# Sums over the partitions as two single-pass products in a hybrid decoder trunk, with the first values kept in DRAM

## What is computed

```python
for l in range(DEPTH):
    h = rms_norm(x, norm_g[l]).astype(x.dtype)
    p = h @ w_in[l]
    z, p_rw, p_ml, p_mla, p_da = _split(p, IN_WIDTHS)
    v_res = None if l == 0 else (rw_v0[l - 1], rw_v_dn[l - 1], rw_v_up[l - 1])
    y_rw, v_first = rwkv7_group(p_rw, v_first, rw_mu[l], ...)
    y_ml = mlstm_group(p_ml, ...)
    y_mla = mla_group(p_mla, ...)
    y_da = diff_attn_group(p_da, l, ...)
    y = jnp.concatenate([beta[0] * y_rw, beta[1] * y_ml, beta[2] * y_mla, beta[3] * y_da], axis=-1)
    y = y * jax.nn.silu(z.astype(jnp.float32))
    x = x + (y.astype(x.dtype) @ w_out[l]).astype(x.dtype)
```

## Time and profile before

| what | value |
|---|---|
| time, median of 3 runs (range) | 2308.97 us (2307.95 to 2311.85) |
| span of the profiled execution | 2306.3 us |
| PE busy | 2270.2 us, 98% |
| POOL busy | 1744.8 us, 76% |
| DVE busy | 1079.8 us, 47% |
| ACT busy | 662.4 us, 29% |
| granted PE clock | 0.998 of full speed |
| mean DMA rate | 125 GB/s |

### The profile page before, as it was taken

One profiled execution on the slowest core, in us unless ns is written; L12 is line 12 of the kernel. 1 busy time (PEld: TensorE's weight loads), 2 busy tenths in 40 slices (PEclk: granted clock), 3 DMA queues, 4 the chain that ended last, 5 costly groups with the idle time before them and its releaser, 6 DMA issues. The chain is left out here.

```text
span 2306.3 us, 38356 instructions
## 1 busy us (share of the span) xinstructions
PE 2270.2 (98%) x16032; PEld 1736.0 (75%) x16032; DVE 1079.8 (47%) x1411; ACT 662.4 (29%) x1193; POOL 1744.8 (76%) x1228
## 2 busy tenths in 40 slices
PE   7999999999999999999999999999999999999999
PEld 5767777777777778777777677767777777777777
DVE  5023337456463762555250232465474547626542
ACT  5222222222221332443341233222132213314421
POOL 3677679678587999888537666886696789898884
PEclk9999999999999999999999999999999999999999
DMA  4722344333234545733445232523332345466333
GB/s 161 191 85 78 108 142 118 92 96 105 81 108 135 160 150 174 252 91 78 146 114 165 82 105 78 174 86 95 94 115 89 88 156 158 135 201 225 90 82 124
DMA packets 165487, 288.64 MB, mean 125 GB/s; under 512 B 28792, under 2 KB 36344, under 8 KB 163776
## 3 DMA queue, kind: packets, MB, share of 16 engines
q1 hardware_dynamic: 125216, 211.60, 31.4%
q10 hardware_dynamic: 40096, 74.57, 9.9%
HBM read 234.43 MB, written 51.68 MB: 124 GB/s over the span
## 5 line engine op out<-in xcount | busy, mean ns | idle before, releaser
L752 POOL TENSOR_SCALAR w_hi<-raw 128x512 fp32r<-128x512 f32 x552 | 908.1, 1645 | 360.9 <-PE ps_proj L793 311.8
L762 POOL TENSOR_TENSOR w_lo<-raw,w_hi 128x512 fp32r<-128x512 f32 (+1 forms) x640 | 842.4, 1317 | 153.5 <-ACT w_hi L1247 98.1
L793 PE MATMUL ps_proj<-h_hi,w_hi 128*128 128x512 f32 (+1 forms) x1760 | 726.1, 413 | 5.1 <-ACT stage L1240 2.4
L793 PE MATMUL ps_proj<-h_lo,w_hi 128*128 128x512 f32 (+1 forms) x1760 | 688.9, 391 | 0.0
L793 PE MATMUL ps_proj<-h_hi,w_lo 128*128 128x512 f32 x1728 | 675.4, 391 | 0.0
L793 PEld LDWEIGHTS ps_proj<-h_hi,w_hi 128*128 128x128 f32 (+1 forms) x1760 | 329.6, 187 | 101.0 <-issue 22.4
L793 PEld LDWEIGHTS ps_proj<-h_lo,w_hi 128*128 128x128 f32 (+1 forms) x1760 | 329.4, 187 | 73.5 <-DVE h_lo L1769 0.2
L793 PEld LDWEIGHTS ps_proj<-h_hi,w_lo 128*128 128x128 f32 x1728 | 325.8, 189 | 66.2 <-issue 7.7
L808 PE MATMUL ps_proj<-w_hi,h_hi 128*128 128x512 f32 x448 | 181.0, 404 | 0.4 <-POOL w_lo L762 0.4
L808 PE MATMUL ps_proj<-w_hi,h_lo 128*128 128x512 f32 x448 | 174.8, 390 | 0.0
L808 PE MATMUL ps_proj<-w_lo,h_hi 128*128 128x512 f32 x448 | 174.6, 390 | 0.0
(11 more groups left out here) (349 smaller groups left out, 2972.1 us busy)
## 6 DMA issues: line engine op xcount, KB each, us to landing
raw<-in_w_in_dram SPq DMA_DIRECT2D x480, 256.0 KB, 2.7
raw<-in_w_out_dram SPq DMA_DIRECT2D x128, 256.0 KB, 3.1
projected<-stage SPq DMA_DIRECT2D x116, 256.0 KB, 2.6
arena<-projected ACTq DMA_DIRECT2D x90, 256.0 KB, 3.1
out_dram<-arena ACTq DMA_DIRECT2D x7, 1024.0 KB, 4.7
gated_hi<-arena ACTq DMA_DIRECT2D x24, 256.0 KB, 2.7
gated_lo<-arena ACTq DMA_DIRECT2D x24, 256.0 KB, 3.2
h_hi<-gated_hi SPq DMA_DIRECT2D x8, 768.0 KB, 5.9
```

What stands on the lines that cost most here:

```text
L752: nc.gpsimd.tensor_scalar(hi, src, 1.0, None, ALU.mult).then_inc(s_hi_split, 1)
L762: nc.gpsimd.tensor_tensor(lo, src, hi.bitcast(F32), ALU.subtract).then_inc(s_raw_split, 1)
L793: last = mm(ps_proj[rows, m, :], lhsT, rhs, start=(k == 0 and j == 0), stop=(k == KT - 1 and j == len(products) - 1))
```

## The change

1. Each sum over the partitions is done on a high and a low half. The operand x is rounded to fp32r as `sq_hi`, the remainder x - `sq_hi` is `sq_lo`, and two fp32r products with fp32r ones (`sum_of_halves`) replace one fp32 product. DVE makes both halves in five of the eight kinds of sum (cast and subtraction), in the other three ACT squares the bank a second time straight into `sq_hi` and DVE subtracts. `sq_hi` and `sq_lo` exist once.
2. The latent norms' squares are first added on DVE, so that one fp32 product each is left of three and two.
3. `v_first` moves from SBUF to DRAM. ACT stores it in layer 0 and loads one pair's part (`rw_vf`) along with r and k in layer 1. DVE's copy to it is gone.
4. `FILL` gets larger numbers at the places in front of the new sums, and mLSTM gets a new place `ml_sq` between its two sums. The number of tiles in all is unchanged, so what is put in earlier is missing at a later place: `to_k` has 29 tiles where it had 37, `to_z_da` none instead of 28, `to_dav` none instead of 9, the rest of the layer 22 (layer 1: 23) instead of 32.

```diff
-    begin=4, la_first=36, la_sums=18, la_v=4, la_heads=(7, 7, 7, 7), la_qk=(18, 11, 13, 11),
+    begin=4, la_first=36, la_sums=18, la_v=4, la_heads=(9, 9, 9, 9), la_qk=(18, 11, 13, 11),
...
-    rw_first=8, rw_lora=(13, 11, 11, 11), rw_factors=(26, 28, 28, 28), rw_turned=(5, 5, 5, 5),
+    rw_first=8, rw_lora=(14, 13, 13, 13), rw_factors=(26, 28, 28, 28), rw_turned=(5, 5, 5, 5),
...
-    rw_carried=(3, 3, 3, 3), rw_gate=(13, 14, 13, 12),
-    ml_first=25, ml_qk=(19, 6, 13, 13), ml_s=(8, 8, 8, 8), ml_h=(3, 3, 3, 3), ml_gate=(0, 0, 9, 0), ml_rest=(22, 15, 6, 12),
+    rw_carried=(5, 5, 5, 5), rw_gate=(13, 14, 13, 12),
+    ml_first=25, ml_qk=(19, 6, 13, 13), ml_s=(8, 8, 8, 8), ml_h=(5, 5, 5, 5), ml_sq=(4, 4, 4, 4), ml_gate=(0, 0, 9, 0), ml_rest=(22, 15, 6, 12),
...
-    da_osq=(3, 4, 3, 3), da_gate=(9, 8, 9, 10))
+    da_osq=(5, 6, 5, 5), da_gate=(9, 8, 9, 10))
...
+                    def sum_of_halves(bank, exact):
+                        mm(bank, exact[:], sq_hi[:], start=True, stop=False)
+                        return mm(bank, exact[:], sq_lo[:], start=False, stop=True)
...
-                    for j in range(3):
-                        mm(ps[:, 0, :], ones, la_sq[:, j, :], start=(j == 0), stop=(j == 2))
-                    for j in range(2):
-                        mm(ps[:, 1, :], ones, la_sq[:, 3 + j, :], start=(j == 0), stop=(j == 1))
+                    mm(ps[:, 0, :], ones, la_sq[:, 0, :], start=True, stop=True)
+                    mm(ps[:, 1, :], ones, la_sq[:, 3, :], start=True, stop=True)
...
-                        pe.wait_ge(s_ml_s_ready, 2 * h + 2)
-                        mm(ps[:, 1, :], ones, ml_sum, start=True, stop=True).then_inc(s_ml_den_mm, 1)
-                        pe.wait_ge(s_ml_squares, 2 * h + 1)
-                        mm(ps[:, 2, :], ones, ml_sq, start=True, stop=True).then_inc(s_ml_h_sum, 1)
+                        pe.wait_ge(s_ml_s_ready, 3 * h + 2)
+                        sum_of_halves(ps[:, 1, :], ones_r).then_inc(s_ml_den_mm, 1)
+                        fill("ml_sq", h)
+                        pe.wait_ge(s_ml_s_ready, 3 * h + 3)
+                        sum_of_halves(ps[:, 2, :], ones_r).then_inc(s_ml_h_sum, 1)
...
                     fill("to_k")
+                    if not mixes_v:
+                        act.wait_ge(s_rw_v_shifted, 1)
+                        act.dma_start(v_first.rearrange("j p t -> p j t"), rw_v[:, :, 1:T + 1]).then_inc(s_rw_first_loaded, 16)
                     act.wait_ge(s_rw_shifted, 1)
...
                         act.wait_ge(s_ml_den_mm, h + 1)
+                        nc.scalar.activation(sq_hi[:], ps[:, 0, :], ACT.Square).then_inc(s_ml_squares, 1)
                         nc.scalar.activation(ml_den, ps[:, 1, :], ACT.Square, scale=EPS ** 0.5).then_inc(s_ml_squares, 1)
+                        fill("ml_sq", h)
...
-                        v.tensor_tensor(rw_sq, rw_kk, rw_kk, MUL).then_inc(s_rw_kk_sq, 1)
+                        link(v.tensor_tensor(rw_sq, rw_kk, rw_kk, MUL))
+                        link(v.tensor_copy(sq_hi[:], rw_sq))
+                        v.tensor_tensor(sq_lo[:], rw_sq, sq_hi.ap().bitcast(F32), SUB).then_inc(s_rw_kk_sq, 1)
...
-                        else:
-                            link(v.tensor_copy(v_first[:, hp, :], vv))
...
+                        link(v.tensor_copy(sq_hi[:], ml_sum))
+                        v.tensor_tensor(sq_lo[:], ml_sum, sq_hi.ap().bitcast(F32), SUB).then_inc(s_ml_s_ready, 1)
+                        dve.wait_ge(s_ml_squares, 3 * h + 2)
+                        v.tensor_tensor(sq_lo[:], ml_sq, sq_hi.ap().bitcast(F32), SUB).then_inc(s_ml_s_ready, 1)
                         if h < HEADS - 1:
                             convolve(h + 1)
...
                         gate(12 + h, 3, da_z, da_e, da_yo, da_o)
+                        if h < HEADS - 1:
+                            split_k_squares(h + 1)
```

More of the change, by code:

```diff
@@ L290, in planned @@
             place("to_z_ml", through=G_Z_ML)
-        for name in ("ml_h", "ml_gate", "ml_rest"):
+        for name in ("ml_h", "ml_sq", "ml_gate", "ml_rest"):
             place(name, h)
@@ L345, in build @@
         small = sb("small", [P, 80])
-        v_first = sb("v_first", [P, 4, T])
+        sq_hi = sb("sq_hi", [P, T], F32R)
+        sq_lo = sb("sq_lo", [P, T], F32R)
+        ones_r = sb("ones_r", [P, P], F32R)
+        bones_r = sb("bones_r", [P, P], F32R)
         stage = sb("stage", [P, 4, T])
-        ARENA = 24528
+        ARENA = 24928
         arena = sb("arena", [P, ARENA])
@@ L381, in build @@
         y_lo_dram = nc.dram_tensor("gated_lo", (EARLY_K, P, T), F32, kind="Internal").ap()
+        v_first = nc.dram_tensor("v_first", (4, P, T), F32, kind="Internal").ap()
         rows_dram = nc.dram_tensor("gate_rows", (HEADS, 2, T), F32, kind="Internal").ap()
@@ L932, in _ @@
                         pe.wait_ge(s_la_squared, 2 * h + 2)
-                        mm(ps[:, 0, :], ones, la_hsq[:, 2, :], start=True, stop=True)
+                        sum_of_halves(ps[:, 0, :], ones_r)
                         pe.wait_ge(s_la_squared, 2 * h + 3)
@@ L1209, in _ @@
                         fill("da_osq", h)
-                        pe.wait_ge(s_da_osq_ready, h + 1)
-                        mm(ps[:, 1, :], ones, da_osq, start=True, stop=True).then_inc(s_da_osum_mm, 1)
+                        pe.wait_ge(s_da_osq_ready, 3 * h + 3)
+                        sum_of_halves(ps[:, 1, :], ones_r).then_inc(s_da_osum_mm, 1)
                         fill("da_gate", h)
@@ L1459, in _ @@
                     act.dma_start(rw_in[:, 1, 1:T + 1], p_dram[4 * G_K]).then_inc(s_rw_rk_loaded, 16)
+                    if mixes_v:
+                        act.dma_start(rw_vf, v_first[0]).then_inc(s_rw_rk_loaded, 16)
                     act.wait_ge(s_ml_gates, 1)
@@ L1544, in _ @@
                     act.wait_ge(s_y_kept, 32 * 8)
+                    if not mixes_v:
+                        act.wait_ge(s_rw_first_loaded, 16 * (rw_loads + 1))
                     fill("to_mlo")
@@ L1665, in _ @@
                         act.wait_ge(s_pv_done, HEADS + h + 1)
+                        nc.scalar.activation(sq_hi[:], ps[:, 0, :], ACT.Square).then_inc(s_da_osq_ready, 1)
                         nc.scalar.activation(da_osq, ps[:, 0, :], ACT.Square).then_inc(s_da_osq_ready, 1)
@@ L1959, in _ @@
                     dve.wait_ge(s_y_kept, 32 * 8)
+                    if not mixes_v:
+                        dve.wait_ge(s_rw_first_loaded, 16 * (rw_loads + 1))
                     v.memset(ml_in[:, :, 0:3], 0.0).then_inc(s_ml_cleared, 1)
@@ L2034, in _, with split_k_squares @@
                     dve.wait_ge(s_da_first_loaded, 16)
+                    def split_k_squares(h):
+                        dve.wait_ge(s_da_squared, 2 * h + 1)
+                        link(v.tensor_copy(sq_hi[:], da_sq[:, 1, :]))
+                        v.tensor_tensor(sq_lo[:], da_sq[:, 1, :], sq_hi.ap().bitcast(F32), SUB).then_inc(s_da_squared, 1)
+                    split_k_squares(0)
                     for h in range(HEADS):
```

48 lines of the change are left out of this document (32 added, 16 removed).

## The result

The changed kernel takes **2438.3 us** (median of 4 runs, 2435.3 to 2441.3); the kernel before took 2308.5 us beside it. The ratio is 1.0558, with a 95% interval of 1.0546 to 1.0570: slower by 5.6%. The direction was forecast, the size was not: 2381 us (2345 to 2405) had been predicted, 57 us too few.

The account below looks back on a forecast made before the run. PE, busy 98%, was taken to bound the kernel by what its instructions take. Span 2306.3 - 32.0 gained + 104.1 lost = 2378.4 us; the median lies 2.7 above, giving 2381 us (2345 to 2405).

Parts of the forecast that it names:

- into RWKV, both layers: Latent attention to RWKV: longer DVE/ACT chain under less cover, 13.8 us in layer 0, 7.4 in layer 1, 21.2 together.
- mLSTM's scores, head 3: mLSTM: the next head's convolution starts later, so head 3's scores wait about 2 us per layer, 4.0 us.
- DAQ: Group now ending in ml_rest of head 0, behind ACT's tanh: PE waits 7.3 and 6.6 us for copies, 13.9 together.
- DAK and what follows it: Group now ending in ml_qk of head 2: PE waits for ACT's copies 5.2 us, in layer 1 2.4, together 7.6.
- DAV: Differential head 0: group ends in da_half without a tile before the first output tile, less cover: 2.0 us (up to 5).
- The sum: Whole kernel: losses of 104.1 us against a gain of 32.0 on a 2306.3 us span, median 2381 us, 3.1% slower.
- The gain: PE's work: 64 cheaper sums 25.6 us, vanished latent-norm sums 5.2, two avoided waits 1.2, together 32.0 us.
- PE's work alone decides: Rival: moved tiles cover the added operations and ACT is in time at the new ends, 2277 us, faster; chance 10%.
- only the chain into RWKV: Rival: copies do not bind, only the two transitions into RWKV cost 21.2 us, 2298 us, 0.5% faster; chance 4%.
- POOL falls behind: Rival: added DVE operations with SBUF operands hold up POOL, PE waits for w_lo, about 2392 us; chance 9%.
- The moved ends: Column groups end earlier, so PE waits for ACT's bank copies and DVE's additions: 66.3 us together (50 to 80).
- D + 15.2: mLSTM: ACT is free 15.2 us after the denominator's sum ends (D, about 768.59), where it was D + 7.9.

Follow-up runs that it names:

- e6b: The changed kernel with ACT issuing layer 0's store of v_first 30 us later, behind the decay's exponentials: 2435.5 us, ratio 1.0539.
- e10: The kernel before with only DVE's additions of the latent tiles' squares, three fp32 sums a layer gone: 2308.7 us, ratio 0.9997.
- e12: The kernel with halves only at latent heads, RWKV's bonus and variance, its latent-norm additions removed and five fp32 products back: 2303.4 us, ratio 0.9974.
- e1: The changed kernel with the FILL numbers of the kernel before, all else of the change kept: 2353.3 us, ratio 1.0197.
- e2: The kernel before with the changed kernel's FILL numbers, sums still single fp32 products and v_first in SBUF: 2397.8 us, ratio 1.0384.

## Why the prediction was wrong in size

The steps that named waits held. Differences of PE's waits, changed kernel against before, in us:

| term | predicted | measured |
|---|---|---|
| into RWKV, both layers | 21.2 | 15.3 |
| k split | 12.6 | 11.0 |
| mLSTM's scores, head 3 | 4.0 | 9.3 |
| V | 4.1 | 3.9 |
| Z_ML | 10.5 | 8.1 |
| DAQ | 13.9 | 14.8 |
| DAK and what follows it | 7.6 | 10.8 |
| Z_DA | 5.0 | 4.2 |
| DAV | 2.0 | 1.6 |
| output columns | 23.2 | 25.5 |
| sum | 104.1 | 104.5 |

With some small ones PE's waits grew by 111 us. That the sums agree is luck, as single terms are off by up to 5.9 us and the errors cancel: the way into RWKV was put too high, because behind the long wait the next 14 tiles ran at the lower clock and covered DVE's lateness at the following sum (e6b shows that wait, 6.0 us, once the first is gone); mLSTM's scores were put too low. The 1.6 us at DAV the profile puts down to POOL's `w_lo`, which ended 0.02 us behind ACT's last copy, so either would have held PE.

**The step that failed is "The sum".** It charged each wait with its length and PE's work with the rate it has at full clock. What was left out is the granted clock: 46 - 3 = 43 us of the 57 that are missing. I could have known it from the kernel before. Its last wait of 2.2 us, which the prediction had no reason to look at, is followed by a window at half clock (columns as above):

```profile
2257.80:2261.20 3.40, 3.40 (x9) 2.63 (x8) 0.00 (x0) 0.00 (x0) 3.32 (x3) 0.50 0.03 7
```

Nine products in 3.4 us, where there would be 15. The kernel before shows this twice with PE at work, the changed one 23 times. Such a stretch does not follow every wait: the other one of 2.2 us, which ends at 1112, has none behind it.

**The gain was put too high** by 6 us. By this account what is neither waits nor clock fell by 25 us instead of 31: with the added tiles, the waits and the clock taken out, the second sum of each mLSTM head gave 0.06 us instead of 0.4 and the differential k sum 0.16, which makes 4.6 us. With the additions ahead of the latent norms the instructions do go, but PE's time doesn't (e10, e12). The remaining 8 us of the 57 are waits that were not forecast or forecast too short.

**The rivals.** "PE's work alone decides" and "only the chain into RWKV" are out: PE is idle 6% of the span, and copies and additions alone hold it for 67 us. "POOL falls behind" did not decide, as PE waits 5 us for `w_lo` in all, but its mechanism is real: it takes the gain where PE would be faster (e10).

**The moved ends.** Each is confirmed by its own wait, and e1 and e2 confirm that the numbers do it. What I had not drawn from it is that DAQ and DAK need both parts of the change, though the working used both (the moved end and ACT free at D + 15.2 instead of D + 7.9).

## What to carry to other kernels

Charge a long wait of PE with more than its length: here 111 us of waits brought 43 us of work at half rate behind them, and products into a free part of a bank during the waits gave 34 us back without shortening one. Tiles that are put in as cover move every later boundary; look at who has to be there when it comes, before asking whether the cover is long enough. And replace an operation by several on another engine only where that engine's chain has been measured to have slack: of eight kinds of sum in this kernel two are shown to have it (the latent heads' and RWKV's variance), a third, the bonus, is doubtful, and the kernel with halves in these three alone is the fastest, 2303 us.

## Unexpected hardware behaviour

- The granted clock was back at 1.00 only 2.9 to 7.0 us after PE had resumed from its longer waits, although PE was at work (6.7 us behind the longest, in the windows above). It can also fall when PE is at work again: at 1062.3, behind a wait that ended at 1060.5. The length of a wait does not decide alone: one of 1.3 us (at 2315) was followed by a stretch at 0.50, one of 2.8 us (at 2242) by none.
- Small bf16 products of 128 columns, which do nothing useful, hold the clock up: 0.996 with them in the waits, 0.974 without, 0.998 in the kernel before.
- DVE's multiplication of two SBUF operands over 2,560 elements stretches POOL's operation under way from 1.29 or 1.49 us to 2.87 to 4.07 us.
